# High-row products first behind each norm, the second mixer's filler moved towards its start, and a gated row product issued ahead of the convolution's low part

## The reference

```
def hybrid_layer(x, norm_g, w_in, ...):
    h = rms_norm_2(x, norm_g)
    z = h @ w_in
    ...
    o_a = fox_attention(heads(fq, FOX_HEADS), heads(fk, FOX_HEADS),
                        heads(fv, FOX_HEADS), ff + fox_b) * jax.nn.silu(f_gate)
    o_b = conformer_conv(glu_in, conv_w, conv_b, conv_ln_g, conv_ln_b,
                         conv_pw) * jax.nn.silu(c_gate)
    o_c = nsa_attention(...) * jax.nn.silu(n_gate)
    mixed = jnp.concatenate([o_a, o_b, o_c], axis=-1)
    return x + mixed @ w_out
```

## Time and profile before

| | us |
|---|---|
| median of 3 runs | 1635.24 |
| lowest and highest | 1633.99, 1635.32 |
| the profiled execution | 1636.7 |
| its span | 1634.9 |
| PE busy | 1594.5 |
| DVE busy | 951.6 |
| ACT busy | 801.9 |

### The profile page before, as it was taken

One profiled execution on the slowest core, in us unless ns is written; L12 is line 12 of the kernel. 1 busy time (PEld: TensorE's weight loads), 2 busy tenths in 40 slices (PEclk: granted clock), 3 DMA queues, 4 the chain that ended last, 5 costly groups with the idle time before them and its releaser, 6 DMA issues. The chain is left out here.

```text
span 1634.9 us, 23336 instructions
## 1 busy us (share of the span) xinstructions
PE 1594.5 (98%) x8942; PEld 1375.3 (84%) x8942; DVE 951.6 (58%) x1449; ACT 801.9 (49%) x1352; POOL 165.8 (10%) x187
## 2 busy tenths in 40 slices
PE   7999999999999999999999999999999999999897
PEld 6888899988888887888889988878888879878886
DVE  5555475444765545555456544665554688577865
ACT  6444464445364444444355454454443555453642
POOL 0000022211200000000021221120000301010100
PEclk9999999999999999999999999999999999999998
DMA  7666455343555555655546443446665453255421
GB/s 244 207 201 203 147 177 192 131 142 129 168 174 186 182 191 166 196 188 184 183 143 197 155 129 127 150 152 213 206 207 192 152 181 117 78 170 170 143 70 52
DMA packets 76431, 269.63 MB, mean 165 GB/s; under 512 B 8480, under 2 KB 9504, under 8 KB 76320
## 3 DMA queue, kind: packets, MB, share of 16 engines
q1 hardware_dynamic: 76320, 268.14, 49.9%
HBM read 267.06 MB, written 1.05 MB: 164 GB/s over the span
## 5 line engine op out<-in xcount | busy, mean ns | idle before, releaser
L289 DVE TENSOR_TENSOR wlo<-raw,whi 128x1024 fp32r<-128x1024 f32 (+4 forms) x468 | 564.9, 1214 | 414.4 <-ACT whi L283 371.2
L283 ACT ACTIVATE whi<-raw 128x1024 fp32r<-128x1024 f32 (+3 forms) x496 | 508.5, 1034 | 433.2 <-PE bank L339 408.3
L337 PE MATMUL bank<-whi,hh 128*128 128x512 f32 (+4 forms) x1312 | 497.8, 379 | 6.8 <-DVE hl L373 3.7
L339 PE MATMUL bank<-whi,hl 128*128 128x512 f32 (+4 forms) x1312 | 486.4, 371 | 0.0
L338 PE MATMUL bank<-wlo,hh 128*128 128x512 f32 (+4 forms) x1312 | 485.8, 370 | 0.0
L337 PEld LDWEIGHTS bank<-whi,hh 128*128 128x128 f32 x1312 | 248.1, 189 | 49.7 <-DVE hl L373 7.0
L339 PEld LDWEIGHTS bank<-whi,hl 128*128 128x128 f32 x1312 | 247.8, 189 | 40.3
L338 PEld LDWEIGHTS bank<-wlo,hh 128*128 128x128 f32 x1312 | 248.3, 189 | 37.3
L337 PE MATMUL bank<-hh,whi 128*128 128x256 f32 x480 | 142.1, 296 | 0.0
L339 PE MATMUL bank<-whi,gl 128*128 128x512 f32 x352 | 138.7, 394 | 0.0
L338 PE MATMUL bank<-wlo,gh 128*128 128x512 f32 x352 | 137.9, 392 | 0.0
(11 more groups left out here) (295 smaller groups left out, 1672.3 us busy)
## 6 DMA issues: line engine op xcount, KB each, us to landing
raw<-W SPq DMA_DIRECT2D x464, 512.0 KB, 3.3
raw<-W SPq DMA_DIRECT2D x26, 384.0 KB, 3.5
raw<-W SPq DMA_DIRECT2D x8, 416.0 KB, 3.0
tab<-tab SPq DMA_DIRECT2D x6, 384.0 KB, 3.9
raw<-W SPq DMA_DIRECT2D x4, 426.0 KB, 3.1
raw<-W SPq DMA_DIRECT2D x6, 192.0 KB, 2.8
x<-x_in SPq DMA_DIRECT2D x2, 512.0 KB, 5.8
tab<-gains SPq DMA_DIRECT2D x2, 512.0 KB, 4.3
```

The source lines that it names most:

```text
L283: high = act.op(lambda e: e.activation(whi[i][:, 0:w], r[:, 0:w], ACT.Copy), self.landed[c], free)
L289: tok = (low or dve).op(lambda e: e.tensor_tensor(wlo[i][:, 0:w], r[:, 0:w], whi[i][:, 0:w].bitcast(F), ALU.subtract), self.landed[c], hig ...
L337: pe.op(lambda e: e.matmul(dst, ah, bh, start=start, stop=False), *tokens, mark=False)
L339: return pe.op(lambda e: e.matmul(dst, al, bh, start=False, stop=stop), mark=mark)
```

## The change

There are four edits.

1. In `row_group`, for the first four chunks behind a norm, each chunk's products are issued as all those of `hh` first and then those of `hl`. The former wait for the ACT pieces alone (`norm.high`), the latter for the DVE pieces (`norm.ready`). There are as many products as before.
2. In the second mixer `cmp` steps count half a step in `tick`; the prelude advances `main` six times and no longer four; the rate is 20/54 a tick and no longer 22/54; and a step is taken as soon as anything is owed, not when a whole step is.
3. In `conv_out`, the low part `ysl` is emitted one step later than `ysh`, so that other generators can emit between them.
4. Nothing else is added or removed; the order of the instructions on each engine follows from these.

```
-                        for kk in range(k0, k0 + n):
+                        if first:
+                            dst, tsl = got[t][1][:, 0:w], slice(t * 128, (t + 1) * 128)
+                            for kk in range(k0, k0 + n):
+                                ws = slice((kk - k0) * w, (kk - k0 + 1) * w)
+                                mm(dst, hh[:, kk, tsl], ch[:, ws], kk == 0, False, ready, first.high[t, kk // 4],
+                                   got[t][2])
+                                mm(dst, hh[:, kk, tsl], cl[:, ws], False, False)
+                            for kk in range(k0, k0 + n):
+                                ws = slice((kk - k0) * w, (kk - k0 + 1) * w)
+                                tok = mm(dst, hl[:, kk, tsl], ch[:, ws], False, kk == nk - 1, first.ready[t, kk // 4],
+                                         mark=(kk == k0 + n - 1))
+                        for kk in range(k0, k0 + n) if not first else ():
...
-                self.ready[t, n] = low
+                self.high[t, n], self.ready[t, n] = high, low
...
                         st.done(c_, tok)
-                        yield
+                        yield 0.5
...
-                _, low = parts_of(ysh[:, :, :], ysl[:, :, :], tmp, d)
-                yield from pause(2)
+                high = a_copy(ysh[:, :, :], tmp, d)
+                yield
+                low = tt(dve, ysl[:, :, :], tmp, ysh[:, :, :].bitcast(F), ALU.subtract, high, d)
+                yield
...
-            for _ in range(4):
+            for z in range(4):
                 next(decays)
                 next(first)
                 next(main)
+                if z > 1:
+                    next(main)
                 next(taps)
...
             def tick():
-                owed[0] += 22 / 54
-                while owed[0] >= 1 and main_left[0]:
-                    owed[0] -= 1
-                    main_left[0] = next(main, "end") != "end"
+                owed[0] += 20 / 54
+                while owed[0] > 0 and main_left[0]:
+                    step = next(main, "end")
+                    main_left[0] = step != "end"
+                    owed[0] -= 0.5 if step == 0.5 else 1
```

More of the change, by code:

```diff
@@ L393, in row_group @@
             k = 0
+            first = norm
             while k < nk:
@@ L419, in row_group @@
                             yield
-                hold = 1
+                hold, first = 1, None
                 yield
@@ L520, in __init__ @@
                 self.row, self.ready, self.rs_tok, self.first_ms = [[None, None], [None, None]], {}, [None, None], {}
+                self.high = {}
             def col(self, t):
```

## The result

The changed kernel takes 1648.28 us (median of 4 runs, 1645.81 to 1651.00), the kernel before 1634.87 (median of 4, 1633.99 to 1635.32): a ratio of 1.0077, 95% interval 1.0064 to 1.009. By the medians it is 13.4 us slower, where I had forecast 2.5 slower, and it lies outside my range. The profiled execution took 1651.0 us with a span of 1649.2, against 1636.7 and 1634.9 before: 14.3 us more. It is the slowest of the four, so its sum is about 3 us above that of the median.

The account below looks back on a forecast made before the run. PE, busy 98% of the span, was taken as the bound. Norms -5.5, mixer starts +7.0, ends +1.0, edit 3 and clock 0 summed to +2.5 us: 1637.7 us, range 1629 to 1645.

Parts of the forecast that it names:

- the clock: Stretches of PE at 1.2 GHz: moved waits may remove some and bring others, 0 us, from -3 to +4.
- forecast two myself: Second mixer's start: PE waits 2.8 us before the first 256-wide products and 3.3 at unit 1's transposition.
- named a third as possible: In the tail, one wait for a copy behind the convolution's steps on ACT could be up to 3 us.
- The third rival: Each layer gets two three-microsecond stretches at clock 0.50 behind new waits, 1.5 us each: +6, 1643.7 us; chance 0.17.
- counter-evidence: Against the clock rival: 1515.09 in the kernel before, a longer wait without a stretch at the lower clock.
- The norms: Edit 1, eight norms: PE's whole waits for `hl` go, -5.5 us, between -4.5 and -6.
- The mixer's start: Edit 2, second mixer's start: late first chunk and queued exponentials cost 3.5 us a layer, together +7.0, from +2 to +10.
- The second rival: Filler at the second mixer's start is covered, chunk landing by 1336.5: 1629.7 us, between 1626 and 1632; chance 0.26.
- The mixer's end: Edit 2, rounds behind unit 17: lost cover of two 512-wide groups, +0.5 a layer, together +1.
- edit 3: Convolution's output: PE's earlier restart balances values and transposition, +0 within 0.3 us.
- the lost cover: Mixer's end: two more uncovered rounds cost 1.4 us more, partly set against small steps done earlier.
- The sum: Whole kernel: -5.5 + 7.0 + 1.0 + 0 + 0 = +2.5 us, 1637.7 on the median.

Follow-up runs that it names:

- the second one: The changed kernel, all edits, measured again beside the kernel before: ratio 1.0079, +12.9 us; its profiled execution has a span of 1644.0 us.
- the filled waits: The changed kernel with products that nobody reads in its four longest waits of each second mixer, against the kernel before: ratio 1.0029, +4.7 us.
- the opening alone: The kernel before with only six main steps instead of four in the second mixer's opening, rate still 22/54: ratio 1.0055, +9.0 us.
- 5 in another: Edits 1 and 3 alone with unread products in that kernel's own second-mixer waits, against the kernel before: ratio 0.994, -9.8 us.

## Why the prediction was wrong, point by point

**The step that failed is the clock: "0, from -3 to +4".** It measured +9.9 us in the profiled execution (+4.1 in the second one), and 7 to 8 us come back when the waits are filled. The reasoning was that new waits come as old ones go; but the changed kernel has four waits of over 2 us from start to start in each layer where the kernel before has two. Of the four I had forecast two myself, and had named a third as possible. The third rival, at 0.17, was the nearest: it put two stretches a layer at 1.5 us each, +6. There were five a layer: seven more in all than in the kernel before, at 1.4 us each. The sentence of the Trainium skill that I gave to that rival ("TensorE: Matmul & The Clock Gate", "Why this matters for your kernels": gaps bring PE back to half its rate) is what the filled waits bear out: 29.1 us at 0.50 became 8.8. The page speaks of longer gaps than these idle times of 2.0 to 2.9 us; the measurement decides.

My reading of the kernel before was also incomplete. It had a third stretch, which I left out, right behind the wait of 1.93 in the earlier trace rows; the three are 13.7 us long and not 8, and cost 5.8 and not 4:

```profile
1343.00:1346.00 3.00, 3.00 (x15) 3.00 (x15) 1.85 (x5) 3.00 (x9) 0.00 (x0) 0.50 0.82 272
```

So two of its four long waits were followed by a stretch (1342.78 and 1607.51), and two were not (1432.01, and 1515.09 of the earlier trace rows, which I took for counter-evidence), while one stretch, from 1568, had no long wait ahead. In the changed kernel all eight had one in the first profiled execution, and all but the one at 1348.71 in the second. A wait raises the chance of a stretch, it does not fix it.

**The norms: right.** Forecast -5.5; -5.2 in the trace, -5.9 by the run of edit 1 alone. All eight waits went, with a loss of about 0.1 left at each tile.

**The mixer's start: right in sum, and close in its steps.** Forecast +7.0; +7.1 in waits and rest. The chunk landed at 1334.36, which is 1338.7 on the time axis of the kernel before (forecast 1338.2); PE waited 2.92 (2.8); unit 3's scores did not wait noticeably in the first layer, 0.9 in the second (1.7); unit 1's transposition waited 1.97 and, in the second layer, 2.9 (3.3). Besides these, three `cmp` steps waited 2.6 us in all for their own chunks. All of this is one profiled execution; in the second one the first layer's two long waits are 3.76 and 3.08 from start to start, and not 3.14 and 2.13. The opening alone cost 9.0 with its clock. The second rival, that the filler is covered there, is refuted: the point from which it decides was a landing by 1336.5.

**The mixer's end and edit 3: too small.** Forecast +1 and 0; +2.5 together. Unit 18's transposition came to wait 1.99 for its copy, and the output's product 2.26 for `ysl` (2.00 at `oc` before). Both belong to edit 2 and its new rate, under which no 512-wide group is left to cover them: from start to start they are 2.16 and 2.42 with edit 2 alone, but 1.19 and 1.50 with the opening alone, at the old rate. Edit 3 was rightly put at nothing alone (0.9994). I had worked out the lost cover as 1.4 us a layer, close to what was measured, and then set 0.9 of it against small steps done earlier; no row stood behind that part.

**The sum.** -5.2 + 7.1 + 2.5 + 9.9 = 14.3, the spans' difference. Without the last term it is +4.4, inside my range.

Open: why stretches fall behind some waits and not behind others; what parts executions of equal mean clock by up to 5.8 us; how much of edit 1's gain the changed kernel loses to the clock.

## What to carry to other kernels

Where PE is busy 98% of the span, count the new waits of 2 us and more as well as their length, and price each at some 1 to 2 us of lowered clock besides (8 such waits: 15.7 and 9.9 us in two executions, the first with two stretches that no long wait preceded; filling the eight gave back 8.4). A wait that can't be removed can be filled: products that nobody reads, shorter than the wait, gave 8 us in one kernel and 5 in another. An even spread of the filler is no gain by itself; what a stream can bring forward is set by when its first chunk lands and by what stands ahead of its conversion and of its low part on each in-order engine.

## What was not expected of the hardware

Two executions of the same program differed in span by 5.2 us (1649.2 and 1644.0) with nearly equal waits and rest (70.8 and 71.3 us together), through time at the lower clock (45.7 and 29.1 us). And 26 thrown-away products of 512 columns (5.9 us of PE's time in all) made a kernel whose PE is 98% busy 4.5 us shorter.
